# Turning the third tile of x by a scaled identity, and three reorderings in a hybrid S5/mLSTM/MoE step

## The reference

```python
def encoder_step(x, states, params):
    mix, new_states = mixer(rmsnorm(x, norm_mix), ...)       # S5 scan and mLSTM in parallel, gated
    x = x + mix
    x = x + moe(rmsnorm(x, norm_moe), w_router, ...)          # top 4 of 32 experts, clamped SwiGLU
    return rmsnorm(x, norm_final), new_states

def mixer(xn, ...):
    u, q, k, v, o, ig, fg, g_s5, g_ml = split(xn @ w_in)
    y, hr, hi = s5_scan(u, ...)            # 32 groups x 64 complex states
    y_s5 = glu(gelu(y) @ w_s5_glu)
    # mLSTM by chunks of 64 tokens, per head:
    h = num / den; hn = (h - mean(h)) * rsqrt(var(h) + EPS)
    y_ml = (sigmoid(o) * hn * ml_gn) @ w_ml_out
    return (sigmoid(g_s5) * y_s5 + sigmoid(g_ml) * y_ml) @ w_out

def moe(x, ...):
    logits = x @ w_router + b_router
    gates = softmax(top_k(logits, 4))
    # each expert: tokens sorted to it, gate_up, SwiGLU, down, weighted sum back
```

## Time and profile before

| | us |
|---|---|
| median of 3 runs | 1234.87 |
| lowest, highest | 1234.55, 1235.54 |
| profiled execution, its own time | 1235.1 |
| its span (first to last instruction) | 1233.4 |

### The profile page before, as it was taken

The page is one execution under the profiler, slowest core; times in us unless marked ns, Lnnn a source line. Parts: engine busy times, 40 slices in busy tenths (PEclk is TensorE's granted clock), DMA queues, the critical chain, the costliest instruction groups (busy, mean ns, idle before and its releaser), DMA issues.

```text
span 1233.4 us, 21136 instructions
## 1 busy us (share of the span) xinstructions
PE 1217.5 (99%) x7773; PEld 556.6 (45%) x7774; DVE 475.4 (39%) x918; ACT 186.5 (15%) x318; POOL 246.8 (20%) x438
## 2 busy tenths in 40 slices
PE   9999999999999999999999999999999999999997
PEld 7666666778433333333333333333343333333332
DVE  6878967435422222223322222222232222222224
ACT  4741024335201000000000000000000000000002
POOL 2177850000211111111121111111111111111100
PEclk9999999999999999999999999999999999999999
DMA  8324232895999999999999999999999999999995
GB/s 234 103 69 137 88 118 69 270 397 214 358 407 425 426 428 430 429 435 430 429 436 429 435 430 429 435 430 431 434 429 435 430 430 435 429 426 429 427 427 203
DMA packets 61045, 440.51 MB, mean 357 GB/s; under 512 B 11822, under 2 KB 40274, under 8 KB 42612
## 3 DMA queue, kind: packets, MB, share of 16 engines
q1 hardware_dynamic: 59796, 439.50, 86.4%
q10 hardware_dynamic: 1216, 0.56, 0.2%
HBM read 438.18 MB, written 1.87 MB: 357 GB/s over the span
## 4 chain that ended last, share of the span: by engine, by line
PE 69%; DMA 12%; DVE 1%; ACT 0%; issue 0%; SPq 0%; DVEq 0%; ACTq 0%
PE psum L1050 31%; PE psum L1095 15%; DMA big<-in_w_gate_up_dram 12%; PE psum L1014 7%; PE psum L1000 4%; PE psum L605 4%; PE psum L583 3%; PE psum L896 2%; PE psum L1060 1%; PE psum L1081 1%; DVE acc L2045 0%; PE psum L912 0%; ACT big L1342 0%; PE psum L925 0%; PE psum L967 0%
## 5 line engine op out<-in xcount | busy, mean ns | idle before, releaser
L1050 PE MATMUL psum<-big 128*64 128x512 f32 x2048 | 471.9, 597 | 4.5 <-DMA big<-in_w_gate_up_dram 4.4
L1995 DVE TENSOR_TENSOR acc<-acc,psum 128x512 f32<-128x512 f32 (+1 forms) x192 | 123.1, 682 | 572.0 <-PE psum L1014 569.8
L1050 PEld LDWEIGHTS psum<-big 128*64 128x64 f32 x2048 | 137.8, 136 | 306.5 <-issue 284.0
L1095 PE MATMUL psum<-big 128*64 128x512 f32 x1024 | 226.8, 595 | 0.0
L605 PE MATMUL psum<-big 128*128 128x320 f32 x576 | 161.1, 436 | 0.0
L1517 POOL COPY big<-uT 96x64 bf16 x32 | 7.5, 234 | 650.5 <-PE psum L1081 649.9
L1095 PEld LDWEIGHTS psum<-big 128*64 128x64 f32 x1024 | 70.7, 137 | 134.1 <-issue 127.9
L605 PEld LDWEIGHTS psum<-big 128*128 128x128 f32 x576 | 107.5, 190 | 47.9 <-issue 5.5
L1014 PE MATMUL psum<-big 64*128 64x512 f32 (+1 forms) x384 | 106.7, 632 | 0.0
L1391 ACT ACTIVATE big<-big 128x512 f32<-128x512 f32 x32 | 20.2, 631 | 543.1 <-DVE big L2018 543.1
L1526 POOL TENSOR_SCALAR big<-cst,big 128x128 f32<-128x128 f32 x96 | 75.1, 793 | 7.7 <-POOL big L1521 7.7
(11 more groups left out here) (293 smaller groups left out, 840.5 us busy)
## 6 DMA issues: line engine op xcount, KB each, us to landing
big<-in_w_gate_up_dram SPq DMA_DIRECT2D x40, 4096.0 KB, 25.1
big<-in_w_gate_up_dram SPq DMA_DIRECT2D x42, 2048.0 KB, 14.2
big<-in_w_down_dram SPq DMA_DIRECT2D x20, 4096.0 KB, 25.9
big<-in_w_down_dram SPq DMA_DIRECT2D x19, 2048.0 KB, 14.9
big<-in_w_in_dram SPq DMA_DIRECT2D x18, 1024.0 KB, 5.3
big<-in_w_gate_up_dram SPq DMA_DIRECT2D x12, 1024.0 KB, 9.2
big<-in_w_down_dram SPq DMA_DIRECT2D x10, 1024.0 KB, 10.1
big<-in_w_s_glu_dram SPq DMA_DIRECT2D x8, 512.0 KB, 4.4
```

Of the source, the lines that this page charges most:

```text
L1050: mm = pe.matmul(psum[SLOT * hf:SLOT * hf + SLOT, GB + gu, :], xeT[:, 4 * (c % 2) + 2 * k + c // 2, :], hidden(big[:, base:base + FF], hf) ...
L1095: mm = pe.matmul(psum[SLOT * hf:SLOT * hf + SLOT, DB, :], hT[:, m, c, :], big[:, base:base + 512], start=False, stop=(c == DN_CHUNKS - 1 a ...
L1995: v.tensor_tensor(x, x, psum[0:n, CB + hf, :], ALU.add).then_inc(S("added"), 1)
```

## The change

The whole text of the change, without the lines that only move an index:

```diff
-        XT = (2, 6, 4)
+        XT, XT_BACK = (2, 6, 4), 0
+        FRONT, BACK = range(6), range(6, DK)
+        COLUMNS = {0: (XB, 0), 2: (XB, 1), 4: (HB, 0), 1: (XB + 1, 0), 6: (HB, 1), 3: (XB + 1, 1), 5: (HB, 2), 7: (HB, 3)}
+        diagonal = xn[0:TS, 2, 0:TS]
         for c in range(NC):
-            plan[CH_SLOT[c]] += [("chunk", c), ("group_root", c)]
+            plan[CH_SLOT[c]].append(("chunk", c))
+            plan[CH_SLOT[c] + (c == NC - 1)].append(("group_root", c))
 # SP: the three loads of vecs go from here to the head of ScalarE's queue
-            sp.dma_start(vecs[0:8, :], ...)
-            sp.dma_start(vecs[8:12, :], ...)
-            sp.dma_start(vecs[12:16, :], ...)
 # TensorE, project
                 for k in range(kk):
+                    if (j, k) == (0, 4):
+                        pe.wait_ge(S("xnT_ready"), 5)
 # TensorE, start
-                    mm = turn(psum[...], xn[0:n, i, k * P:(k + 1) * P], n)
+                    if i < 2:
+                        mm = turn(dst, xn[0:n, i, k * P:(k + 1) * P], n)
+                    else:
+                        mm = pe.matmul(dst, acc[0:n, i, k * P:(k + 1) * P], diagonal, start=True, stop=True)
 # TensorE, routing
             rows_out(2, 3)
+            x1_turned(2, FRONT, XT[2], 11)
             pe.wait_ge(S("mask_ready"), 2)
             rank(1, 0)
             rank(1, 1).then_inc(S("ranks"), 1)
-            pe.wait_ge(S("x1_ready"), 11)
-            fill(0, 2)
-            x1_turned(2, ALL, XT[2], 12)
-            fill(1, 4)
+            x1_turned(2, BACK, XT_BACK, 12)
+            fill(1, 1)
+            pe.wait_ge(S("xm_ready"), 3)
+            logits(2, FRONT)
             pe.wait_ge(S("xT_ready"), 5)
-            logits(2, ALL).then_inc(S("logits"), 1)
-            fill(1, 1)
+            logits(2, BACK).then_inc(S("logits"), 1)
+            rank(2, 0)
+            rank(2, 1)
 ...
             gather_tiles((0, 1))          # now in the order of COLUMNS
-            rank(2, 0)
-            rank(2, 1)
             pe.wait_ge(S("mask_ready"), 3)
             rank(2, 2).then_inc(S("ranks"), 1)
 ...
-            for k in range(4):
-                for h in range(2):
+            for k in COLUMNS:
+                h, kk = k // 4, k % 4
                 mm = pe.matmul(first_columns(k), xh[...], one2[s64, :], ...)
+                if k == 2:
+                    mm.then_inc(S("ranks"), 1)
             mm.then_inc(S("gathered"), 1)
-            fill(1, 3)
 # ScalarE
-            act.wait_ge(S("inv_last"), 1)
-            nc.scalar.activation(xn[s64, 2, :], acc[s64, 2, :], ACT.Copy, scale=st[s64, 11:12]).then_inc(S("xn_ready"), 1)
 ...
+            act.wait_ge(S("xmT"), 3)
+            act.wait_ge(S("logits"), 2)
+            nc.scalar.copy(xT2[:, 0:6, :], cut(psum[:, XT[2], :], DK, TS)[:, 0:6, :]).then_inc(S("xm_ready"), 1)
             act.wait_ge(S("x1_ready"), 12)
             nc.scalar.activation(psum[s64, SCRB, 256:512], acc[s64, 2, 768:1024], ACT.Square, ...)
 # VectorE, start (every columns() now counts in xnT_ready)
             columns(0, 0, 4)
-            inverse_rms(2, TS, 0)
-            dve.sem_inc(S("inv_last"), 1)
+            inv = inverse_rms(2, TS, 0)
+            v.tensor_scalar(diagonal, ident[0:TS, 0:TS], inv, None, ALU.mult).then_inc(S("xn_ready"), 1)
+            columns(1, 0, 4)
+            columns(2, 0, DK)
             columns(0, 4, DK)
-            columns(1, 0, DK)
-            columns(2, 0, DK)
+            columns(1, 4, DK)
 # VectorE, routing
             last_rest(0)
+            inverse(1)
             residual(2, 0)
             turned_rows(1, ALL, XT[1], 2)
-            inverse(1)
+            first_rest(1)
             residual(2, 1)
-            first_rest(1)
+            last_rest(1)
             choose(1)
+            residual(2, 2)
+            residual(2, 3)
             rank_table(0)
-            residual(2, 2)
+            turned_rows(2, BACK, XT_BACK, 4)
             one_hot(0)
-            residual(2, 3)
             rank_table(1)
             one_hot(1)
             dve.sem_inc(S("p_ready"), 1)
-            turned_rows(2, ALL, XT[2], 3)
             inverse(2)
-            last_rest(1)
             choose(2)
 ...
+            dve.wait_ge(S("ranks"), 5)
+            first_part(0).then_inc(S("xe_ready"), 1)
             do(v.tensor_tensor_scan(cumf[:, 2, 1:], ...))
             do(v.tensor_copy(cum[:, :], cumf[:, 2, :]))
             dve.sem_inc(S("cum_ready"), 1)
             dve.wait_ge(S("gathered"), 2)
-            for n, (h, q) in enumerate(((0, 0), (1, 0), (0, 1), (1, 1))):
-                v.tensor_tensor(dst[:, h, q], src[:, h, q], weight, ALU.mult).then_inc(...)
+            for n in range(1, 4):
+                first_part(n).then_inc(S("xe_first"), 1)
```

More of the change, by code:

```diff
@@ L949, in _ @@
             rank(1, 1).then_inc(S("ranks"), 1)
[L950 to L953 removed]
+            x1_turned(2, BACK, XT_BACK, 12)
+            fill(1, 1)
+            pe.wait_ge(S("xm_ready"), 3)
+            logits(2, FRONT)
             pe.wait_ge(S("xT_ready"), 5)
[L955 to L956 removed]
+            logits(2, BACK).then_inc(S("logits"), 1)
+            rank(2, 0)
+            rank(2, 1)
             def first_columns(k):
[L960 removed]
+                b, at = COLUMNS[k]
+                return psum[:, b, at * SLOT:(at + 1) * SLOT]
             def gather_tiles(tiles):
                 order = [(n, q, i) for n, (q, i) in enumerate(PARTS) if i in tiles]
[L965 removed]
+                for k in COLUMNS:
                     for n, q, i in order:
                         pe.matmul(first_columns(k), parts[:, i, q, k * P:(k + 1) * P], pb[:, i, :],
[L968 removed]
+                                  start=(n == 0 and COLUMNS[k][1] == 0), stop=(n == len(PARTS) - 1), skip_group_check=True)
             pe.wait_ge(S("p_ready"), 1)
@@ L985, in _ @@
             pe.wait_ge(S("p_ready"), 2)
-            pe.wait_ge(S("xm_ready"), 4)
-            for k in range(4):
-                for h in range(2):
-                    s64 = slice(TS * h, TS * h + TS)
-                    mm = pe.matmul(first_columns(4 * h + k), xh[s64, k * P:(k + 1) * P], one2[s64, :],
-                                   start=False, stop=True, skip_group_check=True)
+            pe.wait_ge(S("xm_ready"), 5)
+            for k in COLUMNS:
+                h, kk = k // 4, k % 4
+                s64 = slice(TS * h, TS * h + TS)
+                mm = pe.matmul(first_columns(k), xh[s64, kk * P:(kk + 1) * P], one2[s64, :],
+                               start=False, stop=True, skip_group_check=True)
+                if k == 2:
+                    mm.then_inc(S("ranks"), 1)
             mm.then_inc(S("gathered"), 1)
-            fill(1, 3)
             def gather(need):
@@ L1845, in turned_rows @@
                 if i == 2:
-                    v.tensor_copy(xT2, cut(psum[:, b, :], DK, n)).then_inc(S("xT_ready"), 1)
+                    k0, k1 = ks[0], ks[-1] + 1
+                    v.tensor_copy(xT2[:, k0:k1, :], cut(psum[:, b, :], DK, n)[:, k0:k1, :]).then_inc(S("xT_ready"), 1)
                 else:
@@ L1870, in first_rest @@
                 n = TILES[i][1]
[L1871 removed]
+                dve.wait_ge(S("xm_ready"), i + 1 if i < 2 else 6)
                 if i == 0:
@@ L1995, in add, with first_part @@
                     v.tensor_tensor(x, x, psum[0:n, CB + hf, :], ALU.add).then_inc(S("added"), 1)
-            dve.wait_ge(S("gathered"), 2)
-            src = psum[:, XB:XB + 2, 0:4 * SLOT].rearrange("p h (k q s) -> p h q k s", q=2, s=SLOT)
             dst = xeT.rearrange("p (h k q) s -> p h q k s", h=2, q=2)
             by = nmc[:, 1, :].rearrange("p (h k q) -> p h q k", h=2, q=2)
-            for n, (h, q) in enumerate(((0, 0), (1, 0), (0, 1), (1, 1))):
+            def first_part(n):
+                h, q = n % 2, n // 2
+                b, at = COLUMNS[4 * h + q]
+                src = cut(psum[:, b, at * SLOT:(at + 2) * SLOT], 2, SLOT)
                 weight = by[:, h, q][:, :, None].to_broadcast([P, 2, SLOT])
-                v.tensor_tensor(dst[:, h, q], src[:, h, q], weight, ALU.mult).then_inc(S("xe_ready" if n == 0 else "xe_first"), 1)
+                return v.tensor_tensor(dst[:, h, q], src, weight, ALU.mult)
+            dve.wait_ge(S("ranks"), 5)
+            first_part(0).then_inc(S("xe_ready"), 1)
+            do(v.tensor_tensor_scan(cumf[:, 2, 1:], ones[0:1, 0:NE], cumf[:, (MAXB - 2) % 2, 1:], 0.0, ALU.mult, ALU.add))
+            do(v.tensor_copy(cum[:, :], cumf[:, 2, :]))
+            dve.sem_inc(S("cum_ready"), 1)
+            dve.wait_ge(S("gathered"), 2)
+            for n in range(1, 4):
+                first_part(n).then_inc(S("xe_first"), 1)
             first_rest(2)
```

22 lines of the change are left out of this document (7 added, 15 removed).

## The result

| | median us | lowest, highest | ratio to before |
|---|---|---|---|
| before | 1235.05 | 1234.55, 1236.31 | |
| the changed kernel | 1298.47 | 1296.87, 1299.56 | 1.0508 [1.0497, 1.052] |

Forecast were 1232.3 us, a range of 1231.0 to 1234.3, and a chance of 0.05 for slower. The profiled execution has a span of 1297.0 us.

A forecast was written before the change was run, and what follows sets the result against it. In the expert loop TensorE and the weight stream were both taken to be at their limit, so savings ahead of it count in full: +1.0 - 1.4 - 2.2 = -2.6, giving 1232.3 us, range 1231.0 to 1234.3.

The forecast's parts named there:

- Rival D: Routing, s5_columns and before the loop: fewer fills let TensorE's clock fall to 1.2 GHz; slower, 1236.3 us; chance 0.05.
- the forecast's 0.53: Whole kernel: chance given to the forecast, own range 1231.6 to 1233.2 us, half of it beyond the 0.2% line.
- Term 1: Start, third tile: VectorE's new column order delays the S5 arithmetic, so TensorE stalls at s5_columns; +1.0 us.
- Rival C: Start: the eight products take four times the transposes' 0.71 us, 2.84 instead of 1.11; 1234.0 us; chance 0.06.
- Term 2: Middle, last chunk's root: moved behind projection 35's read-out, so projection 37 follows 36 without a gap; -1.4 us.
- Term 3: Routing ahead of the expert loop: reordered steps let the first expert product start earlier; -2.2 us.
- Rival B: Expert loop: the weight stream doesn't follow the earlier start, keeping 1 us or less of the routing's saving; 1233.5 us; chance 0.14.

The follow-up runs named there:

- the start part alone: Kernel before with only the change's start part (scaled identity for the third tile, new column order, moved small-vector loads): 1237.19 us, ratio 1.0016.
- The routing part alone: Kernel before with only the change's routing part (reordered work ahead of the expert loop): 1234.75 us, ratio 0.9992.

## Why the prediction was wrong

**The step that failed** is the sentence on the expert loop: "the diff touches neither, and the loop can only be moved as a whole". The diff moved the loop in TensorE's code as well as in time, by 20 instructions, and the code's place has a price of its own. It is 1298.5 - 1235.1 (the changed kernel less 24 instructions) = 63.3 us, 9.0 for each return. I counted the nine lost fillers and the doubled passes as work and never as code. Shown by six runs: two with the change's text and more instructions or fewer (fast), one without the change and 20 fewer (slow), one a whole packet further (slow), one 12 further (fast), one with a shorter body (fast). That the body touches eight packets is worked out from its length, the good and bad places, and the second stop, which moved by one instruction with the loop; no view shows which packet a fetch brings.

Rival D named the clock as the way to slower. The clock did fall to 0.50, not where D looked for it, and as a follower: TensorE first stood for its code. In the changed kernel less 24 instructions, poorer still in fillers, it was 0.999 in the mean. What D described did happen once, in the kept trace of the kernel with 20 increments (0.71 from 25 to 30 us, some 1.5 us lost), and it is small beside the refetch.

Two readings of the prediction were wrong without a part in this. 32 blocks of 28.19 us from 312.25 end at 1214.3, not at 1220.7; the blocks up to 876 took 28.2 us and the later ones 28.7. And half of the forecast's 0.53 is 0.27, so faster by over 0.2% should have had 0.37 and not 0.48.

**Term 1, start: +1.0 predicted; alone it was 2.15 at s5_columns, 2.33 at the loop's start and 1.6 at the end.** The direction and the mechanism hold; s5_columns waited for VectorE. The size failed at "that form took 1.11 us for 16 at 310.13". In the changed kernel:

```profile
8.86 1.04 PE L584 MATMUL psum<-cst,big 128*128 128x128 f32 x8
9.73 0.83 PE L839 MATMUL psum<-big 128*128 128x128 f32 x6
10.50 2.00 PE L851 MATMUL psum<-big,acc 64*128 64x64 f32 x16
12.53 1.89 DVE L1564 TENSOR_TENSOR big<-psum,vc 128x512 f32<-128x512 f32 x3 [1.90 <-PE psum L851]
```

The row that I borrowed has the same shape, count and type, and other partitions: its products read the two halves by turns, these all the lower one. 2.00 for 1.11 is 0.9 us of what was missing. Rival C's 2.84 us was too high by 0.84, the row too low by 0.89; the answer lay midway (2.00 is 2.8 times the transposes' 0.71). The products also began later than the 9.95 that I had worked out: at 10.23 in the start part alone, where the 0.17 us ahead of the small vectors' turning had stayed. So the first projection began at 13.06 and not at 11.9, and TensorE was 1.1 us late itself before it stood 1.14 us for VectorE.

In the changed kernel the products began at 10.50, right behind the fillers. There the third tile of x landed later, by this row of ScalarE (7.36 before and 7.30 in the start part alone, without a wait for a transfer):

```profile
7.70 1.06 ACT L1144 ACTIVATE big<-acc 64x1024 f32<-64x1024 f32 x1 [0.66 <-DMA acc<-in_x_sample_dram]
```

But that was hidden, as predicted: the scaled identity was ready at 9.67. What came late was TensorE. Its 19 fillers from 3.24 on took 4.11 us, in the start part alone 2.88, so that the first tile was turned from 7.18 and not from 6.90; why the fillers took longer isn't known (the granted clock was 1.00 in both). The order of the columns was priced rightly, three operations of 0.6 us behind the third tile.

**Term 2, middle: -1.4 predicted, -1.5 in the trace, -1.45 in the runs.** Projections 36 and 37 are one unbroken row, and the root stands behind its table load:

```profile
209.01 4.47 PE L608 MATMUL psum<-uT,big 128*128 128x320 f32 x16
209.52 1.28 ACT L1238 ACT_TABLE_LOAD   x1
210.82 0.20 ACT L1238 ACTIVATE sm<-sm 128x2 f32<-128x2 f32 x1
211.04 1.28 ACT L1159 ACT_TABLE_LOAD   x1
213.32 0.38 PE L584 MATMUL psum<-cst,big 128*128 128x128 f32 x2
```

The turn that stood at 212.47 before comes at 213.32, 0.85 later, with a start 2.36 later: 1.51 saved.

**Term 3, routing: -2.2 predicted, -2.2 at the loop's start, -0.9 to -1.1 at the end.** The steps came as written: the logits behind ScalarE's copy, the gather, one rank product, the counts, the first column part. In the changed kernel:

```profile
304.30 0.48 ACT L1378 COPY big<-psum 128x384 f32<-128x384 f32 x1
...
310.48 0.29 DVE L2013 TENSOR_TENSOR big<-psum,sm 128x128 f32<-128x128 f32 x1
310.92 3.65 PE L1059 MATMUL psum<-big 128*64 128x512 f32 x16 [0.39 <-DVE big L2013]
...
312.89 6.69 SPq L435 DMA_DIRECT2D big<-in_w_gate_up_dram  x4
```

The turning of tile 1's sum, before and then in the changed kernel:

```profile
293.87 1.09 PE L583 MATMUL psum<-cst,acc 128*128 128x128 f32 x8
```

```profile
294.73 1.09 PE L584 MATMUL psum<-cst,acc 128*128 128x128 f32 x8
```

It stands 0.86 later, the first expert product 1.33 earlier than at 312.25, the issue of weights 1.33 earlier than at 314.22: 2.2 for both. What I left out is what is late next in the loop's first block, VectorE behind its gate tables: every trace with the routing part has that wait of 0.4 us at the second combine.

```profile
319.64 1.13 PE L1023 MATMUL psum<-big 64*128 64x512 f32 x4 [0.42 <-DVE acc L2002]
```

(The routing part alone moved the loop by only 1.8 from the turning on, since TensorE's last rows of tile 2 were read 0.4 later; why isn't known.)

**Rival B** was half right: the stream is a bound close behind TensorE, as the shorter body shows, and it gives back 0.7 of a delay. But of the savings it took no share that the runs can tell (the root's 1.45 came through); of what the routing lost, 0.4 went to VectorE, and the rest is within the noise.

**Without the refetch** the terms of the trace add to +2.4 - 1.5 - 2.2 + 0.4 = -0.9. The kernel with the whole change and 24 instructions less, which lacks six filler products besides, measured 1235.14 beside 1235.29, no change. So the forecast would have missed its 1232.3 by 2 to 3 us even in a good place: the change's start costs what its routing brings. Left out, it gives the 1233.0 above.

## What to carry to other kernels

An edit ahead of a loop changes where the loop's code lies; count instructions added and removed ahead of it (fillers are instructions too), and look at the count of instruction packets before anything else when a time jumps and the stops say "issue" at the loop's return. Either place such a loop or make its body shorter: by the count above, one of at most 1537 instructions can't touch eight packets (31 fewer were enough at the one place tried). A row is a price for another operation only if the partitions that it reads, and their order, are the same too; and a gain ahead of a loop is to be followed into its first block on every engine.

## What the runs showed of the hardware that was not expected

- A loop of 1559 instructions on TensorE was fetched anew in every pass from some places, 9 packets and about 9 us for each return; from others it fetched none. Good starts: 3743, 3751, 3779, 3787, 3803; bad: 3767, 3768, and 3767 + 256. All agree with this: over seven packets of 256 instructions the body stays, over eight it doesn't.
- TensorE stood twice at each such return, at the loop's head (2.35 us at the first return) and where the next packet begins, 12 instructions on (3.60 us).
- A stop for code costs more than itself: after 5.95 us of standing sixteen products took 7.1 us in place of 3.6, at a granted clock of 0.50 to 0.72.
- A semaphore increment at the head of TensorE's stream costs about 0.15 us: the first filler began at 3.94 us behind 20 of them and at 40.26 behind 256.
- Sixteen records of one form, 64 rows, 64 columns, float32, took 1.11 us with alternating halves of the partitions, 1.60 with one half after the other, and 2.00 on one half alone. On one half a record starts 112 ns behind the last; records on different halves can start 6 or 7 ns apart.
- VectorE stood 2.3 us at its loop's entry before and 2.5 after, with no semaphore shown: nothing before, and 0.4 us of TensorE's time once TensorE came early.
